# Two transformer blocks on one core: one 512-column pass of the high weights in the down and output projections

## What is computed

```python
x = x + 0.5 * swiglu(rmsnorm(x, norm_ffn1), gate, up, down)   # down0, down1: (silu(..)*(..)) @ w_down
x = x + merged @ w_out                                         # wout
x = x + g2 * swiglu_2(h, w_gate, w_up, w_down)                 # down2, down3
```

## Time and profile before

| | us |
|---|---|
| median of three runs | 1226.67 |
| profiled execution | 1227.34 |
| its span, first to last instruction | 1225.4 |
| PE busy (matmul) | 1181.0 (96%) |
| DVE busy | 905.2 (74%) |
| ACT busy | 637.2 (52%) |
| POOL busy | 106.9 (9%) |

### The profile page before, as it was taken

How to read it: one execution, slowest core, us unless ns; L and a number is a source line. 1 busy time by engine, 2 the same in 40 slices (tenths; PEclk the granted TensorE clock), 3 DMA queues, 4 the chain that set the end, 5 groups by cost and what they waited for, 6 DMA issues and landing times.

```text
span 1225.4 us, 23733 instructions
## 1 busy us (share of the span) xinstructions
PE 1181.0 (96%) x9696; PEld 1149.3 (94%) x9696; DVE 905.2 (74%) x1589; ACT 637.2 (52%) x1053; POOL 106.9 (9%) x146
## 2 busy tenths in 40 slices
PE   6999999988999999999999999999999998999999
PEld 5999999977889999999987889999998888999999
DVE  4689988465367899997979778888657777666643
ACT  5554555434464654444656654545447785544541
POOL 1000002022100100000455210000100001000000
PEclk8999999989999999999999989999999999999999
DMA  6597878542236588989742357778653434565552
GB/s 247 180 316 250 316 301 311 187 155 82 91 121 180 184 297 302 310 305 347 268 142 74 104 172 259 260 257 299 230 166 113 138 121 146 167 190 187 176 187 86
DMA packets 70524, 251.92 MB, mean 206 GB/s; under 512 B 7824, under 2 KB 9616, under 8 KB 70416
## 3 DMA queue, kind: packets, MB, share of 16 engines
q1 hardware_dynamic: 70416, 250.41, 61.0%
HBM read 249.33 MB, written 1.05 MB: 204 GB/s over the span
## 4 chain that ended last, share of the span: by engine, by line
PE 83%; DVE 11%; ACT 2%; issue 2%; POOL 1%; DMA 1%; SPq 0%; POOLq 0%; DVEq 0%; ACTq 0%
PE ps L471 25%; PE ps L475 25%; PE ps L472 25%; DVE wlo L958 2%; PE ps L567 1%; PE ps L462 1%; ACT s L1747 1%; PE ps L560 1%; PE ps L465 1%; PE ps L466 1%; DVE hlo L975 1%; PE ps L601 1%; DMA raw<-w_stream 1%; PE ps L897 1%; DVE s L1349 1%
## 5 line engine op out<-in xcount | busy, mean ns | idle before, releaser
L471 PE MATMUL ps<-hhi,whi 128*128 128x256 f32 (+1 forms) x1968 | 568.1, 289 | 7.2 <-DVE hlo L975 6.2
L475 PE MATMUL ps<-hhi,wlo 128*128 128x256 f32 (+1 forms) x1968 | 558.2, 284 | 1.0 <-DVE wlo L958 0.8
L472 PE MATMUL ps<-hlo,whi 128*128 128x256 f32 (+1 forms) x1968 | 557.8, 283 | 0.0
L958 DVE TENSOR_TENSOR wlo<-raw,whi 128x1024 fp32r<-128x1024 f32 x373 | 454.3, 1223 | 23.9 <-ACT whi L1517 23.2
L1517 ACT ACTIVATE whi<-raw 128x1024 fp32r<-128x1024 f32 x373 | 386.1, 1048 | 61.6 <-DMA raw<-w_stream 39.3
L471 PEld LDWEIGHTS ps<-hhi,whi 128*128 128x128 f32 x1968 | 374.7, 190 | 15.6 <-issue 14.3
L475 PEld LDWEIGHTS ps<-hhi,wlo 128*128 128x128 f32 x1968 | 374.8, 190 | 1.7 <-DVE wlo L958 1.3
L472 PEld LDWEIGHTS ps<-hlo,whi 128*128 128x128 f32 x1968 | 375.7, 191 | 0.3
L475 PE MATMUL ps<-hidhi,wlo 128*128 128x256 f32 x704 | 196.1, 279 | 0.0
L471 PE MATMUL ps<-hidhi,whi 128*128 128x256 f32 x704 | 196.1, 279 | 0.0
L472 PE MATMUL ps<-hidlo,whi 128*128 128x256 f32 x704 | 196.1, 279 | 0.0
(11 more groups left out here) (216 smaller groups left out, 1257.1 us busy)
## 6 DMA issues: line engine op xcount, KB each, us to landing
raw<-w_stream SPq DMA_DIRECT2D x373, 512.0 KB, 4.5
raw<-ada_in SPq DMA_DIRECT2D x96, 512.0 KB, 4.8
out_dram<-vx SPq DMA_DIRECT2D x8, 128.0 KB, 2.4
con<-con_in SPq DMA_DIRECT2D x1, 962.0 KB, 6.1
raw<-w_stream SPq DMA_DIRECT2D x2, 256.0 KB, 3.4
vx<-x_in SPq DMA_DIRECT2D x2, 256.0 KB, 6.2
cond<-c_in SPq DMA_DIRECT2D x1, 512.0 KB, 4.4
vx<-x_in SPq DMA_DIRECT2D x3, 128.0 KB, 4.1
```

The source lines that it names most:

```text
L471: e.matmul(bank, wh, r_hi, start=i == FIRST[o] and not shared, stop=False, skip_group_check=True)
L472: e.matmul(bank, wh, r_lo, start=False, stop=False, skip_group_check=True)
L475: mm = e.matmul(bank, wl, r_hi, start=False, stop=i == LAST[o], skip_group_check=True)
L958: e.tensor_tensor(wlo[:, n % RING, :], raw[:, slot, :], whi[:, n % RING, :].bitcast(F32), ALU.subtract).then_inc(lo_done, 1)
```

## The change

High and low parts that had tensors of their own now lie side by side in one: `w2` for the weights (high and low of a chunk), `h2`, `hidp`, `mgp`, `y1p`, `o2p`, `o3p` for the operands (for an input tile, first the 256 high columns, then the 256 low ones; 258 each in `h2`). The old names are views of them. In the stages of `HALVED` the high weights of a tile meet both parts in one matmul of 512 columns, whose result fills both halves of a bank: the product with the high operand in columns 0 to 255, that with the low operand in 256 to 511. The low weights add to the first half. The three-matmul form stays for all other stages. `residual` adds the second half of the bank to x first, waits for that on a semaphore of DVE's own, and then adds the first half as before. The diff, without the renamed tensors and the operands that return the pair instead of two parts:

```diff
+HALVED = ("down0", "wout", "down1", "down2", "down3")
...
-        whi = sb("whi", [P, RING, CW], F32R)
-        wlo = sb("wlo", [P, RING, CW], F32R)
+        w2 = sb("w2", [P, RING, 2, CW], F32R)
+        whi, wlo = w2[:, :, 0, :], w2[:, :, 1, :]
...
-        hhi = sb("hhi", [P, KD, S + 2], F32R)
-        hlo = sb("hlo", [P, KD, S + 2], F32R)
+        h2 = sb("h2", [P, KD, 2, S + 2], F32R)
+        hhi, hlo = h2[:, :, 0, :], h2[:, :, 1, :]
...
-            hidhi = sb("hidhi", [P, KF, S], F32R, scope)
-            hidlo = sb("hidlo", [P, KF, S], F32R, scope)
+            hidp = sb("hidp", [P, KF, 2, S], F32R, scope)
+            hidhi, hidlo = hidp[:, :, 0, :], hidp[:, :, 1, :]
...
+                    elif o[0] in HALVED:
+
+                        if half:
+                            e.wait_ge(hi_done, c + 2)
+                        e.matmul(bank.rearrange("p (i t) -> p i t", i=2), wh, r, start=i == FIRST[o], stop=False, skip_group_check=True)
+                        if half:
+                            e.wait_ge(lo_done, c + 2)
+                        mm = e.matmul(bank[:, 0:S], wl, r[:, 0, :], start=False, stop=i == LAST[o], skip_group_check=True)
+                        at[0] = i + 1
...
-                    return ps[:, res_bank(r, m)[0], 0:S]
+                    return ps[:, res_bank(r, m)[0], :]
...
+                if r not in (3, 5):
+                    v_step.mark(e.scalar_tensor_tensor(x[:, m, :], ps[:, b, S:2 * S], coef(r, m), x[:, m, :], ALU.mult, ALU.add))
+                    e.wait_ge(v_step.sem, v_step.n)
                 e.scalar_tensor_tensor(x[:, m, :], ps[:, b, o:o + S], coef(r, m), x[:, m, :], ALU.mult, ALU.add).then_inc(x_new, 1)
```

More of the change, by code:

```diff
@@ L267, in two_blocks @@
             with ExitStack() as inner:
-                mghi = sb("mghi", [P, KD, S], F32R, inner)
-                mglo = sb("mglo", [P, KD, S], F32R, inner)
+                mgp = sb("mgp", [P, KD, 2, S], F32R, inner)
+                mghi, mglo = mgp[:, :, 0, :], mgp[:, :, 1, :]
                 mg = sb("mg", [P, 2, 2, S], F32, inner)
@@ L274, in two_blocks @@
             gr = sb("gr", [P, 2, KD, S], F32, scope)
-            y1hi = sb("y1hi", [P, 6, S], F32R, scope)
-            y1lo = sb("y1lo", [P, 6, S], F32R, scope)
+            y1p = sb("y1p", [P, 6, 2, S], F32R, scope)
+            y1hi, y1lo = y1p[:, :, 0, :], y1p[:, :, 1, :]
             bias1 = sb("bias1", [P, BIASES, S], F32, scope)
@@ L289, in two_blocks @@
             pT2 = sb("pT2", [P, 2, 2, 3 * P], F32, scope)
-            o2hi = sb("o2hi", [P, KD, S], F32R, scope)
-            o2lo = sb("o2lo", [P, KD, S], F32R, scope)
+            o2p = sb("o2p", [P, KD, 2, S], F32R, scope)
+            o2hi, o2lo = o2p[:, :, 0, :], o2p[:, :, 1, :]
             st2 = sb("st2", [P, KD, 32], F32, scope)
@@ L304, in two_blocks @@
             trir = sb("trir", [P, P], F32R, scope)
-            o3hi = sb("o3hi", [P, KD, S], F32R, scope)
-            o3lo = sb("o3lo", [P, KD, S], F32R, scope)
+            o3p = sb("o3p", [P, KD, 2, S], F32R, scope)
+            o3hi, o3lo = o3p[:, :, 0, :], o3p[:, :, 1, :]
             st3 = sb("st3", [P, 2, 4], F32, scope)
@@ L454, in tiles @@
                     bank = begin(o, i == FIRST[o])
-                    r_hi, r_lo = operand(o, kt)
-                    if j == 0 or i == CH // 2 and c == 0:
-                        e.wait_ge(hi_done, c + 2 if i else 1)
+                    r = operand(o, kt)
+                    half = j == 0 or i == CH // 2 and c == 0
+                    wh, wl = (w[:, c % RING, j * P:(j + (2 if o[0] in PAIRED else 1)) * P] for w in (whi, wlo))
                     if o[0] in PAIRED:
-                        wh, wl = (w[:, c % RING, j * P:(j + 2) * P] for w in (whi, wlo))
+                        if half:
+                            e.wait_ge(hi_done, c + 2)
                         for tt in range(2):
-                            b, x_hi, x_lo = bank[:, tt * S:tt * S + S], r_hi[:, tt * P:tt * P + P], r_lo[:, tt * P:tt * P + P]
+                            b, x_hi, x_lo = bank[:, tt * S:tt * S + S], r[:, 0, tt * P:tt * P + P], r[:, 1, tt * P:tt * P + P]
                             e.matmul(b, x_hi, wh, start=kt == 0 and tt == 0, stop=False, skip_group_check=True)
-                            if j == 0 and tt == 0:
+                            if half and tt == 0:
                                 e.wait_ge(lo_done, c + 2)
@@ L467, in tiles @@
                         at[0] = i + 2
+                    elif o[0] in HALVED:
+                        if half:
+                            e.wait_ge(hi_done, c + 2)
+                        e.matmul(bank.rearrange("p (i t) -> p i t", i=2), wh, r, start=i == FIRST[o], stop=False, skip_group_check=True)
+                        if half:
+                            e.wait_ge(lo_done, c + 2)
+                        mm = e.matmul(bank[:, 0:S], wl, r[:, 0, :], start=False, stop=i == LAST[o], skip_group_check=True)
+                        at[0] = i + 1
                     else:
-                        wh, wl = (w[:, c % RING, j * P:(j + 1) * P] for w in (whi, wlo))
                         shared = o[0] in ("wo2", "wo3") and o[1] % 2 == 1
-                        e.matmul(bank, wh, r_hi, start=i == FIRST[o] and not shared, stop=False, skip_group_check=True)
-                        e.matmul(bank, wh, r_lo, start=False, stop=False, skip_group_check=True)
-                        if j == 0 or i == CH // 2 and c == 0:
+                        if half:
+                            e.wait_ge(hi_done, c + 2 if i else 1)
+                        e.matmul(bank, wh, r[:, 0, :], start=i == FIRST[o] and not shared, stop=False, skip_group_check=True)
+                        e.matmul(bank, wh, r[:, 1, :], start=False, stop=False, skip_group_check=True)
+                        if half:
                             e.wait_ge(lo_done, c + 2 if i else 1)
-                        mm = e.matmul(bank, wl, r_hi, start=False, stop=i == LAST[o], skip_group_check=True)
+                        mm = e.matmul(bank, wl, r[:, 0, :], start=False, stop=i == LAST[o], skip_group_check=True)
                         at[0] = i + 1
@@ L490, in operand @@
                             e.wait_ge(sh_lo, s - 2)
-                    return hhi[:, kt, 0:n], hlo[:, kt, 0:n]
+                    return h2[:, kt, :, 0:n]
                 return operand
@@ L552, in operand @@
                         e.wait_ge(hid_lo, n * KF + kt + 1)
-                    return hidhi[:, kt, :], hidlo[:, kt, :]
+                    return hidp[:, kt, :, :]
                 tiles(c0 + 22 * CH, begin, operand)
@@ L685, in operand @@
                     n = kt + (2 if o[0] == "upb" else 0)
-                    return y1hi[:, n, :], y1lo[:, n, :]
+                    return y1p[:, n, :, :]
                 tiles((C0["up"] + 6) * CH, begin, operand)
@@ L696, in begin @@
                         e.wait_ge(mg_sum, (5, 6, 8, 7)[m // 2])
-                    return ps[:, (4 + m) % 8, 0:S]
+                    return ps[:, (4 + m) % 8, :]
                 def operand(o, kt):
@@ L703, in operand, with heads_product @@
                         e.wait_ge(mg_lo, kt + 1)
-                    return mghi[:, kt, :], mglo[:, kt, :]
+                    return mgp[:, kt, :, :]
                 tiles((C0["wout"] + 8) * CH, begin, operand)
-            def heads_product(r, o_hi, o_lo, hi_ok, lo_ok, free):
+            def heads_product(r, heads, hi_ok, lo_ok, free):
                 seen = set()
@@ L722, in operand @@
                         e.wait_ge(lo_ok, kt + 1)
-                    return o_hi[:, kt, :], o_lo[:, kt, :]
+                    return heads[:, kt, :, :]
                 return begin, operand
@@ L746, in free @@
                         e.wait_ge(du2, 9)
-                products = heads_product(3, o2hi, o2lo, o2_hi, o2_lo, free)
+                products = heads_product(3, o2p, o2_hi, o2_lo, free)
                 def upto(tick, tile=0):
@@ L859, in free @@
                         e.wait_ge(zm3, 16)
-                products = heads_product(5, o3hi, o3lo, o3_hi, o3_lo, free)
+                products = heads_product(5, o3p, o3_hi, o3_lo, free)
                 def upto(tick, tile=0):
```

## The result

The changed kernel takes 1234.55 us, the median of four runs (1233.79 to 1237.99), beside 1226.32 for the kernel before (1225.47 to 1228.54) on the same chip. The ratio is 1.007, with a 95% interval of 1.0047 to 1.0093. The profiled execution took 1234.5 with a span of 1232.6, 7.2 us more than the span of before.

What follows compares the result with a forecast made beforehand. The prediction took the kernel as a stream of PE matmuls with places where DVE sets the time. Adds of 5.35 us less 1.5 gained on PE gave +3.9 on the median of 1226.67: 1230.6 us, range 1221.3 to 1236.

Steps and rivals of the forecast that it cites:

- the likeliest case: Whole kernel: second adds cost 5.35 us, matmuls gain 1.5, net +3.9, 1230.6 us; chance 0.50.
- the second rival: Wide matmul stalls more the longer it is, 237 to 240 ns from start to start; 1236 us; chance 0.12.
- signs of being wrong: Boundaries behind wout and down1 do not grow, or the tiles change by more than 5 ns.
- 2.4 us behind wout: Second adds delay DVE by 3.5 us, with room of 1.1 before PE needs the diagonal of ffn1's norm.
- 2.45 in or behind down1: Second adds delay DVE by 3.5 us, with room of 1.05 before PE takes up the sum of squares.
- 0.5 at the end: After the last matmul the store waits for a second residual add, with nothing beside it: 0.5 us.
- The adds hidden in down0 and down2: DVE room of 2.4 us against 1.8 in down0, about 8 against 4.1 in down2: no cost.
- the gain of the matmuls: Wide matmul at 224.3 or 233.3 ns replaces two narrow ones in five stages: 1.5 us gained together.
- a turn of pace: A changed stage may switch between the two paces: 4.4 ns for each of 352 matmuls, 1.5 us per down stage.
- The first: Wide matmul has only the fixed overhead, 215.5 ns; gains 10.6 against 5.35, 1221.4 us; chance 0.25.
- The third, hidden adds: DVE's second adds are hidden; 0.5 at the end against 1.8 of gain, 1225.4 us; chance 0.13.
- The layout: Normed operand's row step goes from 1032 to 2064 bytes: priced at nothing, 2 us either way.

Runs made afterwards that it cites:

- e3_wide: Changed kernel with the 512-column matmul but only one residual add, the second half of the bank left out of x; 1231.42 us, 1.0032 of the kernel before.
- e2_adds: New layout with three 256-column matmuls, the low-operand product in the second half of the bank, two adds per output; 1229.0 us, 1.0012 of the kernel before.
- e4_room: Changed kernel with wide matmul and second add only in down0, down2, down3; wout and down1 narrow with one add; 1229.24 us, 1.002 of the kernel before.
- e7_rows: Changed kernel with the 42 modulation rows between ffn1 and mix2 ten chunks sooner; 1237.12 us, 1.0073 of the kernel before.
- e1_layout: Kernel before with the new layout alone, still three 256-column matmuls and one add; 1222.59 us, 0.9964 of the kernel before.
- e11_h2: Kernel before with only the normed operand's high and low parts side by side; 1221.15 us, 0.9946 of the kernel before.
- e12_half: New layout, narrow matmuls, one add, but outputs 4 to 7 of down0, down2, down3 wide with two adds; 1224.97 us, 0.9991 of the kernel before.
- e6_pad16: New layout, narrow matmuls, one add, normed operand rows padded from 258 to 272 columns, bias ring 4 instead of 5; 1231.94 us, 1.0034 of the kernel before.

## Why the prediction was right, and where it was off

*The direction and the place of the stops* were right, and the time fell within the range of 1221.3 to 1236. But 1234.55 lies outside the 1227.5 to 1233.5 that the likeliest case had for itself; the range held because it was stretched to the second rival, and that is partly luck. One of the prediction's own signs of being wrong came true too: in down0 and down1 the tiles changed by more than 5 ns, by 13. Forecast: 2.4 us behind wout, 2.45 in or behind down1, 0.5 at the end, 5.35. Measured, after against e3_wide, which lacks only the adds: ffn1 +2.70, down1 +1.35, the end +0.51, 4.6. down1 was too high: PE there ran at the slow pace, which leaves DVE more room, and it stopped for chunk 14 where the room had been worked out for chunk 15; where it ran fast (e2_adds) the cost was 1.96 in the stage and 0.4 behind it, close to the 2.45. Behind wout the size was right, but I had looked at the diagonal alone. The longest single stop is for the low operand of output 6, a wait for which I had worked out no room. The adds hidden in down0 and down2 were hidden (e4_room, e3_wide and after: 62.17 to 62.18 us in each).

*The step that was mis-sized* is the gain of the matmuls: "a tile gains 2.4 or 2.3 ns", 1.5 us in all where it counts. Two things were wrong in it. First, the wide matmul took 235 ns, not 224.3 or 233.3: the split of the excess into 2.3 ns fixed and the rest in proportion gave the 384-column rows their 175 from the slow pace, though they stood behind matmuls at the fast one (from which it gives 168.8), and at 512 it failed: the slow pace came out in proportion altogether, 118 for 256 and 235 for 512. A tile gained 0.0 ns against three narrow matmuls at the slow pace. Second, I had let the wide matmul keep the pace of its stage and named a turn of pace as an uncertainty of 1.5 us. That was also too small by a third: it counted 352 matmuls at 4.4 ns, but a tile has three times 256 columns, 528 in a stage. The stream always went to the slow one, 13.4 ns a tile: 2.3 us each in down0 and down1 (e3_wide). So the matmuls cost 4.6 us where I had them gain 1.5. With the 4.6 of the adds that makes 9.2, against 5.35 - 1.5 = 3.9 forecast. This was the point "over 227 ns at the fast pace" from which the second rival decides, and its loss of 10 to 13 ns a tile at the fast pace was met; at the slow pace it was wrong, since nothing was lost there. The result, +8.2 on the medians, lies nearer to its 1236, +9.3, than to my +3.9.

*The rivals.* The first, 215.5 ns and 1221.4 us, did not happen in any of the 26 stages or half stages that ran wide. The rule of the Trainium skill that stands behind it ("TensorE: Matmul & The Clock Gate", section "Back-to-back issue gap", N/2.4 + 2.5 for an isolated matmul at full clock) gives 215.8 ns; the traces here have 225 at the least (e7_rows, once) and 235 as a rule. The third, hidden adds, is refuted by e2_adds against e1_layout.

*The layout* was priced at nothing. With the matmuls and adds kept as they were it takes 0.36% off (e1_layout), mostly from the fast pace in down2 and down3 (2.3 us each) and in wout (0.8), and little from the tiles that read the normed operand (355.9 against 357.5 ns in ffn0 and ffn1, 359.1 against 358.4 in ffn2 and ffn3). In the changed kernel the wide matmul takes the gain in pace away again.

*Open.* What the fast pace is made of. It holds over hundreds of matmuls with every address changing. At the start of down0 it came again in a second execution. It can turn after a wait (wout: 113 ns before a stop of 1.2 us, 118 after it, in the kernel before), after a short one in one execution and not in another (down1). In down2 and down3 it goes with the layout that the stage ahead reads. No experiment here says what of a wait or of the stage ahead decides it, and none changes one of them alone by a few ns.

## What to carry to other kernels

Here a weight load ran beside a matmul, and leaving it out gained nothing (353.4 ns a tile with it and without it): price it from the starts of neighbouring matmuls, not from the 190 ns of its row. Work that a PE saving moves to another engine is paid where that engine has no idle time ahead of something PE waits for; look for that in a window of the stage, and list every wait in it, not the last one only. And before a change is judged by its total, run its layout alone: here the part that looked neutral was the only one with a gain, 1221.15 us for the normed operand alone, against 1228.15 for the kernel before beside it. A pace that one profile shows behind a wait should be looked for in a second profile before it is put down to an edit.

## What the runs showed of the hardware

- A stream of fp32r matmuls of 256 columns at the full granted clock ran at one of two steady paces, 113.3 or 117.8 ns from start to start, over 50 to 176 tiles on end. In down2 and down3 the pace was the same in two executions of a program and changed with the layout of an operand that the stage itself does not read (e11_h2). Behind a short wait in down1 it went on at 113.3 in one execution and at 117.8 in another of the same program, with 153 and 159 ns from the start of the waiting matmul to the next.
- 512 columns took 235 ns (118 x 2) in a steady stream, and 225 to 233 in places, most of them near the start of a stage or behind a wait, and 226 for the first one behind a stream at the fast pace. There the first such matmul ended the fast pace, in three stages of three (e12_half).
- Rows padded to 64 bytes made 256-column reads 0.9 ns a tile faster and 258-column reads 4.2 ns slower (e6_pad16 against e1_layout), in a run that moved other tensors too.
